# Feed-forward down product: seven block products of a 2x2 split in place of a direct product, with operand sums made by GpSimd

## What is computed

```python
h = rms_norm(x, norm_ffn[l])
up = causal_dwconv(h @ ffn_w_up[l], ffn_conv_w[l], ffn_conv_b[l])   # 1024 -> 2 x 2816, conv of width 3
u_val, u_gate = jnp.split(up, 2, axis=-1)
x = x + (jax.nn.gelu(u_gate) * u_val) @ ffn_w_down[l]               # 2816 -> 1024
...
return rms_norm(x, norm_final)
```

## Time and profile before

| | us |
|---|---|
| median of 3 runs (lowest to highest) | 2625.37 (2622.48 to 2629.85) |
| the profiled execution, own time | 2634.46 |
| its span, first to last instruction | 2632.7 |
| TensorE busy in the span | 2482.2 (94%) |
| VectorE, ScalarE, GpSimd busy | 1582.7, 1074.8, 735.1 |

### The profile page before, as it was taken

The page is one execution under the profiler, slowest core; times in us unless marked ns, Lnnn a source line. Parts: engine busy times, 40 slices in busy tenths (PEclk is TensorE's granted clock), DMA queues, the critical chain, the costliest instruction groups (busy, mean ns, idle before and its releaser), DMA issues.

```text
span 2632.7 us, 32946 instructions
## 1 busy us (share of the span) xinstructions
PE 2482.2 (94%) x12224; PEld 2003.0 (76%) x12224; DVE 1582.7 (60%) x2166; ACT 1074.8 (41%) x1847; POOL 735.1 (28%) x648
## 2 busy tenths in 40 slices
PE   7999999999799996995999999899989999989995
PEld 5777777777578775874888888788868888878884
DVE  7554447774355674455777777445577877763435
ACT  6434353332146553213444444225444444432422
POOL 4111103331003770323333333012044534310103
PEclk9999989999899998997999999999999999999997
DMA  4232224442513325364212122365413222225472
GB/s 160 97 111 93 94 87 156 143 148 72 191 59 127 103 71 212 108 228 180 88 72 93 76 88 85 140 211 201 163 73 131 102 88 81 86 83 175 146 242 109
DMA packets 147199, 327.27 MB, mean 124 GB/s; under 512 B 12624, under 2 KB 54624, under 8 KB 139104
## 3 DMA queue, kind: packets, MB, share of 16 engines
q1 hardware_dynamic: 147040, 325.17, 35.4%
HBM read 231.55 MB, written 93.57 MB: 123 GB/s over the span
## 4 chain that ended last, share of the span: by engine, by line
PE 46%; DVE 3%; ACT 1%; DMA 1%; issue 1%; POOL 1%; SPq 0%; DVEq 0%; ACTq 0%; POOLq 0%
PE ff_bank L2035 16%; PE ff_bank L2037 15%; PE ff_bank L2036 15%; DVE ff_y L2618 1%; POOL ffn_rstd L2362 1%; DMA ff_b_raw<-h_t 1%; DVE ff_x2d L2649 1%; DVE ffn_rstd L2645 1%; DMA ff_a_raw<-a_t 0%; ACT ff_y L2457 0%; ACT ff_b_hi L2420 0%; DVE ff_x2d L2640 0%; DVE ff_a_lo L2632 0%; ACT ff_e L2448 0%; ACT ff_ring L2438 0%
## 5 line engine op out<-in xcount | busy, mean ns | idle before, releaser
L2035 PE MATMUL ff_bank<-ff_b_hi,ff_ring 128*128 128x512 f32 x1232 | 483.5, 392 | 37.3 <-DVE ff_ring L2580 15.8
L2036 PE MATMUL ff_bank<-ff_b_lo,ff_ring 128*128 128x512 f32 x1232 | 482.0, 391 | 0.0
L2037 PE MATMUL ff_bank<-ff_b_hi,ff_ring 128*128 128x512 f32 x1232 | 482.0, 391 | 0.0
L66 PE MATMUL ip_bank<-ip_x_hi,ip_w_hi 128*128 128x512 f32 x736 | 309.1, 420 | 19.4 <-DVE ip_x_lo L701 16.2
L2035 PEld LDWEIGHTS ff_bank<-ff_b_hi,ff_ring 128*128 128x128 f32 x1232 | 233.1, 189 | 90.4 <-issue 31.7
L67 PE MATMUL ip_bank<-ip_x_lo,ip_w_hi 128*128 128x512 f32 x736 | 298.8, 406 | 0.0
L68 PE MATMUL ip_bank<-ip_x_hi,ip_w_lo 128*128 128x512 f32 x736 | 297.4, 404 | 0.0
L2035 PE MATMUL ff_bank<-ff_a_hi,ff_w_hi 128*128 128x512 f32 x704 | 276.6, 393 | 15.5 <-DVE ff_a_lo L2632 15.4
L2618 DVE SCALAR_TENSOR_TENSOR ff_y<-ff_u,ff_conv_all,ff_y 128x1024 f32<-128x1024 f32 x176 | 240.2, 1365 | 62.8 <-ACT ff_y L2457 59.3
L2036 PE MATMUL ff_bank<-ff_a_lo,ff_w_hi 128*128 128x512 f32 x704 | 275.7, 392 | 0.0
L2037 PE MATMUL ff_bank<-ff_a_hi,ff_w_lo 128*128 128x512 f32 x704 | 275.4, 391 | 0.0
(11 more groups left out here) (244 smaller groups left out, 4402.2 us busy)
## 6 DMA issues: line engine op xcount, KB each, us to landing
ff_raw<-in_slabs SPq DMA_DIRECT2D x44, 1024.0 KB, 4.8
ff_a_raw<-a_t SPq DMA_DIRECT2D x88, 512.0 KB, 4.1
proj_t<-ip_staged SPq DMA_DIRECT2D x92, 256.0 KB, 2.7
a_t<-ff_y SPq DMA_DIRECT2D x44, 512.0 KB, 2.7
ff_w_raw<-in_w_down SPq DMA_DIRECT2D x88, 256.0 KB, 2.7
rp_tables<-in_rope SPq DMA_DIRECT2D x24, 512.0 KB, 4.5
ip_w_raw<-in_w_in SPq DMA_DIRECT2D x23, 512.0 KB, 4.1
at_qkv<-proj_t SPq DMA_DIRECT2D x12, 768.0 KB, 12.1
```

Of the source, the lines that this page charges most:

```text
L66: pe.matmul(out, w_hi[k], x_hi[k], start=(k == 0), stop=False)
L2035: pe.matmul(out, w_hi, x_hi, start=first, stop=False, skip_group_check=resumed)
L2036: pe.matmul(out, w_hi, x_lo, start=False, stop=False, skip_group_check=resumed)
L2037: return pe.matmul(out, w_lo, x_hi, start=False, stop=last, skip_group_check=resumed)
```

## The change

The up product keeps its own sequence. The down product is changed to seven block products as well: the weights are split in two by output half (m) and by even and odd tile of the 22 (k), the activations by even and odd tile and by block of positions. Each of the seven products runs over eleven tiles (`KP` = 11), 77 steps in a half, and a step is one weight tile 128 x 512 and one activation tile 128 x 512 (256 KB each), 12 matmuls into 4 banks. The sums of the products are built up in two groups of 4 banks, in which a product begins afresh or goes on (`DOWN`: weights, activations, bank group, fresh); six drains (`DRAINS`) and an addition by GpSimd from a copy (`e_down`) of the first product put the results together.

The sums of weight tiles (S1 to S4) and of activation tiles (T1 to T4) are made by GpSimd during the up product, written to memory (`s_t`, `t_t`) and read back in the down product. The weight sums are made once, in the first half. Three raw slots take the place of two, the residual is held whole for both blocks (two loads of 2 MB in a half), `x3_t` is gone, and the norm of block b = 1 is finished before the last steps of the down product.

```diff
-PASSES = 2
-OC = KT // PASSES
+OC = KT // 2
+KP = PAIRS // 2
...
+        DOWN = [("A11", "B11", 0, True), ("A12", "B21", 0, False), ("S2", "T2", 1, True), ("S1", "T1", 0, True),
+                ("S3", "T3", 1, False), ("S4", "B22", 0, False), ("A22", "T4", 1, False)]
+        STEPS = len(DOWN) * KP
+        DRAINS = [(1, 0, 0), (2, 1, 0), (3, 1, OC), (4, 1, OC), (5, 1, 0), (6, 0, OC)]
...
+            def load_sums(i):
+                if i:
+                    sp.wait_ge(sums_stored, 16 * i)
+                for m in range(2):
+                    sp.dma_start(sums[:, 2 * m:2 * m + 2, :], w_down[m, 2 * i:2 * i + 2].rearrange("k p c -> p k c")).then_inc(sums_in, 16)
+            def store_sums(i):
+                sp.wait_ge(sums_made, 4 * (i + 1))
+                sp.dma_start(s_t[i], sums[:, :, :]).then_inc(sums_stored, 16)
+            def store_t(half, g):
...
+                if g % 2 == 0:
+                    sp.wait_ge(t_made, 5 * I + 1)
+                    sp.dma_start(t_t[0, i, :, at], t_sum[:, 0, :]).then_inc(t_stored[0], 16)
+                else:
+                    for t in (1, 2):
+                        sp.wait_ge(t_made, 5 * I + 2 + t)
+                        sp.dma_start(t_t[t, i, :, at], t_sum[:, t, :]).then_inc(t_stored[t], 16)
+                    sp.wait_ge(t_made, 5 * I + 5)
+                    sp.dma_start(t_t[3, i, :, at], t_sum[:, 0, :]).then_inc(t_stored[0], 16)
...
-                if n >= 2:
-                    sp.wait_ge(d_lo_ready, 2 * (N - 1))
+                if n >= 3:
+                    sp.wait_ge(d_lo_ready, 2 * (N - 2))
...
+                for g in range(PAIRS):
+                    if half and g == 1:
+                        store_out(0, 0)
+                    if g + 2 < PAIRS:
+                        load_slab(half, g + 2)
+                    if g == PAIRS - 1:
+                        for n in range(3):
+                            load_step(half, n)
+                    if g:
+                        store_a(half, g - 1)
+                        store_t(half, g - 1)
+                    if half == 0 and g % 2 == 0:
+                        if g:
+                            store_sums(g // 2 - 1)
+                        load_sums(g // 2)
+                for n in range(3, STEPS):
+                    load_step(half, n)
+                    if n == 8:
+                        store_a(half, PAIRS - 1)
+                        store_t(half, PAIRS - 1)
+                        if half == 0:
+                            store_sums(KP - 1)
+                    if n in (11, 13):
+                        load_x(half, (1, 0)[(n - 11) // 2])
+                    if half == 0 and n in (9, 15, 17, 19):
+                        load_piece(1, (9, 15, 17, 19).index(n))
...
+            def sums_of_weights(i):
+                pool.wait_ge(sums_in, 32 * (i + 1))
+                pool.tensor_tensor(sums[:, 3, :], sums[:, 2, :], sums[:, 3, :], ALU.add).then_inc(sums_made, 1)
...
+                pool.tensor_tensor(sums[:, 1, :], sums[:, 1, :], sums[:, 0, :], ALU.subtract).then_inc(sums_made, 1)
+            def sums_of_gated(half, g):
...
+                pool.wait_ge(gated, PAIRS * half + g + 1)
...
+                if g % 2 == 0:
...
+                    pool.tensor_tensor(t_sum[:, 0, :], y_val[:, blk(1)], y_val[:, blk(0)], ALU.subtract).then_inc(t_made, 1)
+                    pool.tensor_copy(t_sum[:, 2, :], y_val[:, blk(1)]).then_inc(t_made, 1)
+                else:
...
+                    pool.tensor_tensor(t_sum[:, 1, :], y_val[:, blk(1)], t_sum[:, 0, :], ALU.subtract).then_inc(t_made, 1)
+                    pool.tensor_tensor(t_sum[:, 2, :], y_val[:, blk(1)], t_sum[:, 2, :], ALU.subtract).then_inc(t_made, 1)
...
+                    pool.tensor_tensor(t_sum[:, 0, :], y_val[:, blk(0)], t_sum[:, 1, :], ALU.subtract).then_inc(t_made, 1)
...
                     if g + 2 < PAIRS:
                         sums_of_slab(half, g + 2)
+                    if g:
+                        sums_of_gated(half, g - 1)
+                    if half == 0 and g % 2:
+                        sums_of_weights(g // 2)
                     if half == 0:
                         save_halo(g, 1)
...
+            def keep_first_product(half):
+                for o in range(OC):
+                    act.wait_ge(down_done, down_count(half, KP - 1, o))
+                    act.activation(e_down[:, o, :], banks[o][:, :], ACT.Copy).then_inc(e_down_ready, 1)
...
+                for n in range(3, STEPS):
+                    if n == KP + 3:
+                        keep_first_product(half)
+                    if 44 <= n < 48:
+                        square(half, n - 44)
+                    if 60 <= n < 64:
+                        square(half, n - 60 + OC)
+                    if n == 70:
+                        for t in range(2 * OC, 3 * OC):
+                            square(half, t)
+                    if n == 73:
+                        root(half, 1)
+                    high_step(half, n)
...
+                    if n == 73:
+                        invert(half, 1)
+                        scale_late(half, 1, (0, 1))
+                    if n == 74:
+                        scale_late(half, 1, (2, 3))
...
                 for n in range(STEPS):
+                    if n == 69:
+                        sum_squares(half, 1)
                     down(half, n)
             sum_squares(1, 0)
-            sum_squares(1, 1)
```

More of the change, by code:

```diff
@@ L2471, in high_step @@
[L2471 to L2484 removed]
+                act.wait_ge(d_in[n % 3], 32 * loads_of(half, n))
```

470 lines of the change are left out of this document (256 added, 214 removed).

## The result

The kernel became slower, by 0.8%. In seven runs each, the changed kernel took 2654.73 us (2649.62 to 2660.42) and the kernel before 2633.92 on the same chip: a ratio of 1.0082 (95%: 1.0066 to 1.0097). The forecast was 2571, 2545 to 2610; it started from 2625.4 for the kernel before, the median of its first three runs.

What follows compares the result with a forecast made beforehand. TensorE's matmuls were taken to bound all four product stretches. 2634.5 - 59.8 - 2.3 - 11 + 7 + 18 - 6 = 2580.4 us for the profiled execution, or 2571 us against the median; range 2545 to 2610.

Steps and rivals of the forecast that it cites:

- Removed matmuls: Down products: 924 matmuls each instead of 1056, at 0.2265 us each, 59.8 us less if operands arrive in time.
- GpSimd's sums in the up product: First up product: GpSimd's added operations slow VectorE and SyncE's queue delays slabs; 18 us more, from 0 to 45.
- The ring: First up product: GpSimd's work and SyncE's stores and loads wait in turn; 38.9 us against 38.1 for two pairs.
- the slower rival: First up product: sums at 1.98 us each make the kernel slower, 2663 us; decides from 1.76 us an operation; chance 0.07.
- Contention: First up product: GpSimd's extra operations slow VectorE's taps and low part, costing 0.8 us for each two pairs.
- The same in the second half: Second up product: GpSimd's extra operations slow VectorE's taps, about 0.4 us a pair over 21 pairs, 7 us more.
- Waits in the down product: Both down products: 22.3 us of old waits go, 20 us of new ones come; -2.3 us, from both sides 8 to 40.
- Step 3: Start of each down product: VectorE's low parts come late at steps 2 and 3, 3 us of waiting.
- The residual and next operands: Down products: extra loads in eleven steps delay operands, 0 to 8 us; 3 taken in the first half, 1 in the second.
- Norm and steps 73 to 75: Late down product: early norm at step 69 costs 2 us; reciprocal and scalings make low part 75 late, 3 us.
- The third rival: Down products become DMA-bound, smaller pieces moving at only 220 GB/s; 2619 us, no change; chance 0.07.
- Between the halves: From first down to second up product: shorter wait for `move`, 3 of 13.9 us lost kept; -11 us (-14 to 0).

Runs made afterwards that it cites:

- e1: Changed kernel with SyncE's queue reordered in the first up product: weight sums stored before operand sums, their tiles loaded earlier, behind the slab; median 2619.86 us.
- e3: Changed kernel without the weight sums' stores and loads and without GpSimd's 44 weight-sum operations, plain weight tiles read instead; 2598.36 us.
- e4: Changed kernel without any weight or operand sums, their copies or stores; the down product reads plain tiles instead; 2585.63 us.
- e5_x_later: Changed kernel with the two 2 MB residual loads issued before steps 16 and 22 of the down product, not 11 and 13; 2670.19 us.
- e6: Changed kernel with the edits of e1 and e5_x_later, and the first product copied before step 13's high parts; median 2628.89 us, 0.9983 of the kernel before.
- e8: e1 with the residual and the next operands of the down product loaded in 256 KB pieces spread over the steps; 2612.34 us.
- e2: Changed kernel without the weight sums' memory traffic (one load, no stores), GpSimd still doing the operations; 2613.7 us.

## Why the prediction was wrong, point by point

**Removed matmuls, -59.8.** Right. Each down product has 924, and in the middle of the second the clock is at 1.00 and a matmul costs what was assumed: its excess stays at 14.8 to 14.9 us from matmul 336 to 756.

**GpSimd's sums in the up product, +18 in the first half: this step failed.** It measured +58.5: 36.8 for the queue's order (e1), 18.8 for the weight sums on GpSimd (e3) and 2.9 for the operand sums (e4). The mechanism was named, ring and contention both, but the sizes were off:
- *The ring.* It was put at 38.9 us against 38.1 and measured 44.6 in the round shown, 43.2 as the stretch's mean (475.0 / 11). The queue's part was right: 14 foreseen, 13.4 measured. What was wrong is GpSimd's part, 24.9 foreseen and 31.2 measured. "About 1.5 us each" for the added operations was 1.6 to 2.1: weight sums 1.74, operand sums 2.00 (81.8 us / 41); the slab sums, put at 1.6, took 1.61 (122.4 / 76). Over the seventeen operations of two pairs (eight, four, four, and a copy of 1.6) the mean is 1.73, next to the 1.76 from which the slower rival was said to decide. That rival, given 0.07, had the mechanism: at 1.73 us an operation its formula gives a ring of 14 + 27.7 + 1.6 = 43.3. That its 2663 lies near the measured 2654.73 is in part luck, since it has nothing of the 33.5 us by which the down products missed. By e1 the ring cost 37 us: it was more than "just about closed".
- *Contention.* It was put at 0.8 us for two pairs, from the chain around the taps, 1.4 us of whose slack it was set against. The operations slow nearly everything in which VectorE reads two operands from SBUF, its low parts above all, and e3 and e4 give that 18.8 and 2.9 us of stretch: 2 us for two pairs. A share of 282 / 388 had looked like ample room; with the operations stretched it became 394 / 438.

So a range of 0 to 45 went over: two causes, of which one feeds the other (operations slowed by contention close the ring), were priced as a sum of small terms. "A first up stretch over 435 us" was named as the sign of being wrong on the slow side, and it came (475.0).

**The same in the second half, +7.** Right to a few us. By matmul 168 of the second up product the excess is 11.3 us, and 6.5 come after; before 15.3 and 2.8. So +3.7, and e3 against e4 gives the operand sums 5.1 in all.

**Waits in the down product, -2.3: the second step that failed.** Excess rose from 12.3 + 10.0 to 35.2 + 18.3, +31.2 us, of which e4 leaves 22.7 with no sums made. By its terms:
- *Step 3, 3 us*: measured 3.47 and 3.50. Right.
- *The residual and next operands, 3 and 1 us (0 to 8)*: one wait of 7.83 at step 11 and 6.44 in the second half, and in the first one of 1.9 ahead of it and a train of shorter ones behind it (2.2, 1.0, 1.4 at steps 16 to 25): 14.3 and 6.4. What failed is "loads run six steps ahead" (16 us). Three raw buffers let a load run three steps, 8.2 us, ahead of the low parts, and steps 6 to 10 had their loads issued 10.2 to 11.9 us ahead of their first matmul, four steps. The second 2 MB load took 13.3 us from issue to landing, and step 12's operand, behind the first, 11.9. The copy of the first product, which the timeline under e5_x_later shows tied to step 13's operand, had no term at all. The stretch of these loads in the first down product:

```profile
1745.00:1762.60 17.60, 15.44 (x67) 12.06 (x66) 5.18 (x8) 4.61 (x8) 0.00 (x0) 1.00 1.03 376
1762.60:1800.00 37.40, 27.35 (x109) 21.55 (x108) 22.76 (x22) 11.76 (x22) 20.71 (x14) 0.86 0.84 295
```

The DMA engines are full at 376 GB/s first, and then TensorE idles. e5, e6 and e8 agree: moving the loads moves the stall, and cutting them up shrinks it in the second half.
- *Norm and steps 73 to 75, 2 + 3 us*: somewhat dear. Over the last 168 matmuls the excess grows by 4.2 us in the first half and 3.4 in the second: at step 69, with the matmul with ones, 1.9 and 1.0, and one wait of 1.66 at step 74.
- *The clock, which had no term.* In the second down product the waits over 0.6 us are 3.50, 6.44 and 1.66, 11.6 us, and the excess 18.3. Of the other 6.7 us, 4.2 lie in 20 matmuls that start about 0.43 us apart, at the lower granted clock, and 1.0 at step 69. In the first down product, in the second row above, the clock averages 0.86, between its two levels of 2.4 and 1.2 GHz, around and behind the wait of 7.83 us. Such matmuls cost 5.7 and 4.2 us in the two down products, for 3.0 and 1.8 in the kernel before. The forecast had seen this in the kernel before and then counted each new wait at its bare length.

The third rival (the down product bound by DMA) was right for the steps around the large loads and wrong for the stretch: 0.68 of the DMA engines over the first down product, 218 GB/s.

**Between the halves, -11.** The excess by matmul 168 fell from 15.3 to 11.3 us, so -4. The wait of 8.6 us is gone, but four of 1.9 to 2.8 stand there now, two of them over the 2 that the forecast allowed, and e4 has 9.7 with no sums. So 7 of the 11 us did not come; what makes these waits was not tested.

**The end, -6.** Right: 26.4 us for 32.6.

Sum of the misses against the forecast's -54.1 us of span: 58.5 - 18 = 40.5 in the first up product, 31.2 + 2.3 = 33.5 in the downs, -0.4 + 4 = 3.6 in the second up with the stretch between the halves, 2.6 ahead of the feed-forward, -0.2 at the end: 80.0, which is 25.9 + 54.1. The 2.6 are scatter: nothing was changed there, and the 25th matmul of the first up product starts between 1240.0 and 1250.1 us in the thirteen traces.

Left open: why a low part beside GpSimd's operations lasts 0.94 us in one kernel and 1.31 in another (no run measures the pair alone), how much of the stall at step 11 an earlier copy would save, the waits at the start of the second up product, and why e5 and e6 lose more than the stall that they move.

## What to carry to other kernels

Where an in-order queue both stores results and loads inputs of the same engine, add up the ring round it, with the durations that the operations have in company and not alone; when the sum is within a few per cent of the period, reorder the queue first (here worth 37 us, for four moved lines). Price GpSimd work by what it does to those operations of VectorE that read two operands from SBUF: 44 operations cost VectorE 55 us, and took nearly all its slack from a share that looked harmless. A large load in front of time-critical ones stalls them for about its duration less what the buffers hold (13.3 less 8.2 us here, where 6 to 8 were measured), and more where other work of the engine is queued behind them. Each stall of TensorE costs its length and then some matmuls at the lower clock. Before reading a difference of 3 us between single runs, look at how far the unchanged stretches differ.

## What was not expected of the hardware

- One and the same low-part operation of VectorE (128x512) took 783, 953, 1143 and 1294 ns on average, by what GpSimd and VectorE themselves had to do beside it, and GpSimd's sums of this size 1.26 to 2.37 us.
- VectorE's operations that read a PSUM bank were not slowed at all: 0.69 us at most in every kernel, beside GpSimd's work or not.
- Work moved from GpSimd to VectorE, where it lasts half as long (899 ns for 1.74 us), gave back only a quarter of what it had cost the stretch (4.5 of 18.8 us): VectorE was then busy 394 of 434 us all the same.
- 21 MB of additional traffic in the first up product changed its stretch by 0.1 us (e1 and e2), while two loads of 2 MB in a down product went with a stop of TensorE of 4 to 9 us in every kernel that had them.
